# The cached keys of a decode unit turned inside the next slot, between the second and third turned group, instead of at a slot's end

## The chip, the cores and the metric

The kernel runs on one core of one Trainium2 chip. Its time is the device time in microseconds. The kernel before took 1446.33 us (median of 3 runs, 1446.19 to 1446.55).

## What is computed

One inference step of one decoder layer, for a prompt of 512 tokens and 8 decode sequences of one token each with 2048 cached positions. The layer is `x + 1/2 FFN`, then `x + Mixer`, then `x + 1/2 FFN`, and a final norm. The change lies in the mixer's attention (heads of 64 values, 8 query heads, 2 key heads):

```python
s = einsum('btghd,btgnkd->btghnk', q, kg) * scale      # selected blocks of cached or new keys
p = softmax(where(ms, s, NEG));  o_sel = einsum('btghnk,btgnkd->btghd', p, vg)
s = einsum('btghd,bkgd->btghk', q, kw) * scale         # sliding window of 512
p = softmax(where(mw, s, NEG));  o_win = einsum('btghk,bkgd->btghd', p, vw)
return gates[..., 0:1] * o_cmp + gates[..., 1:2] * o_sel + gates[..., 2:3] * o_win
```

The same function serves the prompt, whose keys are the new rows, and the samples, whose keys come from the paged caches and the window buffer. Everything is computed in float32.

## The kernel before

The program is written out engine by engine, with semaphores. It runs FFN 1, the mixer's input projection, the attention stage, the mixer's gates and output projection, and FFN 2. The attention stage, from about 684 to 862 us, is where the change lies. Two kinds of work are interleaved there.

**Prompt units.** There are eight, p = 0 to 7 (four head pairs by two branches). For each, TensorE computes scores (`scores`) into fixed banks, VectorE adds the causal mask, takes maxima and writes them to the tile `sm` (`big_scores`, L1297), ScalarE takes exponentials, VectorE makes factors (`factors`, L1313) and scales two small tiles, and GpSimd scales six tiles of `sm` by the factors (`scaled(p)`, L653; 128x512 twice, 128x384 twice, 128x256, 128x128). TensorE then turns (transposes) the scaled tiles in six groups e = 0 to 5 (`turns`, L1707; labels `("tp", p, e)`); ScalarE copies each out (`turned`, L892) to `ptp` or `ptd`, and TensorE multiplies by the value rows (`values`, L1719).

**Sample units.** There are ten, v = 0 to 9 (two window units, eight batches). The cached rows of unit v lie in `GB[v % 2]`. TensorE turns its keys in four quarters of four 128x128 transposes (`sample_keys`, L1741; labels `("kt", v, q)`), each copied to the tile `kt` by ScalarE (quarters 0 and 2, L852) or, from v = 4, by VectorE (quarters 1 and 3, L1290). Then come its scores (`sample_scores`, L1753; label `sc`), VectorE's addition of the selection mask into `sS`, which empties the bank, and the maximum (L1271), ScalarE's exponential, the turning of `sS` (label `pt`), and its product with the values (`sample_values`; label `pv`), which VectorE copies to `oacc` (L1285) after the factors. GpSimd gathers the rows of unit p + 4 from the cache inside `scaled(p)`, after its second tile, once the values of unit p + 2 are done.

**Slots.** The loop over p = 0 to 6 stands on each engine (ScalarE L942, VectorE L1379, TensorE L1838): a slot turns and multiplies prompt unit p, computes scores and factors of p + 1, and handles sample unit p + 3. Each engine does its queue strictly in order.

**The ring.** Banks 5 to 7 of PSUM are shared by all results named by labels, in the order of the list `RING` (L372 to L384). TensorE takes a bank with `claim` (L1685), which waits until the content three places earlier in the list has been copied away (`emptied`). The list has to follow TensorE's order.

Of the kernel before, what the change touches and what calls it, by code (L numbers as in the profile page):

```python
# [120 lines left out]
def build(nc, a):  # L121

    with ExitStack() as ctx:
# [40 lines left out]
        sc = small("sc", [P, 4, 2, DB])  # L164
# [204 lines left out]
        def keys_of(v):  # L369
            return [("kt", v, q) for q in range(4)]  # L370
# [2 lines left out]
                                                                          ("pt", 1), ("pv", 1)]  # L373
        RING += keys_of(2) + [("kc",), ("sc", 2), ("cs", 0), ("cs", 1), ("pt", 2), ("pv", 2)] + keys_of(3)
        for p_ in range(8):
            RING += [("tp", p_, e) for e in range(3)] + ([("sc", p_ + 3)] if p_ < 7 else []) + [("tp", p_, e) for e in range(3, 6)]
            if p_ == 0:
                RING += [("ct", 0), ("ct", 1)]
            if p_ < 7:
                RING += [("pt", p_ + 3), ("pv", p_ + 3)]  # L380
            if p_ < 6:
                RING += keys_of(p_ + 4)
            if p_ == 6:
                RING += [("st",)]  # L384
        RING += [("fw",), ("os",)]
# [295 lines left out]
        def _(act):  # L681
# [170 lines left out]
            def keys(v, quarters):  # L852

                for q in quarters:
                    act.wait_ge(ring_full, full("kt", v, q))
                    if v:
                        act.wait_ge(ring_full, full("sc", v - 1))
                    act.activation(kt[:, q, :], bank[:, rbank("kt", v, q), :], ACT.Copy).then_inc(ring_act, 1)
# [33 lines left out]
            def turned(p, tiles):  # L892

                for e in tiles:
                    act.wait_ge(ring_full, full("tp", p, e))
                    if e == 0 and p:
                        act.wait_ge(pv_done, p)
                    if e == 0 and p == 0:
                        act.wait_ge(ring_full, full("hid"))
                    g, bk = e % 2, rbank("tp", p, e)  # L900
                    for i in ((3,), (2,), (1, 0))[e // 2]:
                        src = bank[:, bk, (2 * P if i == 0 else 0):][:, 0:(i + 1) * P].rearrange("p (k n) -> p k n", n=P)
                        if g == 0:
                            dst = ptp[:, 0:i + 1, (i + 1) * P:(i + 2) * P]
                        else:
                            dst = ptd[:, :, :].rearrange("p k n -> p (k n)")[:, (3 - i) * 5 * P:(3 - i) * 5 * P + (i + 1) * 6 * P]\
                                .rearrange("p (k n) -> p k n", n=6 * P)[:, :, 0:P]
                        ins = act.activation(dst, src, ACT.Copy)
                    ins.then_inc(ring_act, 1)
# [30 lines left out]
                act.activation(oth[:, j, 0:SEQ], bank[:, 4, :], ACT.Copy).then_inc(o_hi, 1)  # L940

            for p in range(7):  # L942
                turned(p, range(4))
                sample_exp(p + 3)
                turned(p, (4, 5))
                if p == 0:
                    for g in range(KVH):
                        act.wait_ge(ring_full, full("ct", g))
                        act.activation(ptc[:, g, :], bank[:, rbank("ct", g), :], ACT.Copy).then_inc(ring_act, 1)
                exps(p + 1, TOPROW)  # L950
                sample_turned(p + 3)
                exps(p + 1, REST)
                if p < 6:
                    keys(p + 4, (0, 2))
                if p % 2:
                    merged(p // 2)
            hi(U_M3)
# [46 lines left out]
            for t in range(QT + 1):  # L1004
                p = P if t < QT else DB
# [6 lines left out]
        def _(dve):  # L1012
# [229 lines left out]
            turned = bank[0:NCMP, 4, 0:2 * P].rearrange("p (b e) -> p b e", e=32)[:, :, 0:NH]  # L1242
# [28 lines left out]
            def sample_scores(v):  # L1271

                k = stat(v)
                dve.wait_ge(ring_full, full("sc", v))
                if v:
                    dve.wait_ge(ring_full, full("pt", v - 1))
                blocks = mk[:, k, 0:NSEL - 1].unsqueeze(1).unsqueeze(3).to_broadcast([P, 4, NSEL - 1, 4])
                tt(sS[:, :].rearrange("p (s k c) -> p s k c", s=4, c=4), bank[:, rbank("sc", v), :].rearrange("p (s k c) -> p s k c", s=4, c=4),
                   blocks, ALU.add).then_inc(ring_dve, 1)
                dve.wait_ge(*emptied("sc", v))  # L1280
                st.did(dve.tensor_reduce(smx[:, k:k + 1], sS[:, :], AX.X, ALU.max))
                st.wait()
                ts(snm[:, k:k + 1], smx[:, k:k + 1], -SCALE, None, ALU.mult).then_inc(s_nm, 1)
# [6 lines left out]
            def keys(v, quarters):  # L1290

                for q in quarters:
                    dve.wait_ge(ring_full, full("kt", v, q))
                    dve.wait_ge(ring_full, full("sc", v - 1))
                    dve.tensor_copy(kt[:, q, :], bank[:, rbank("kt", v, q), :]).then_inc(ring_dve, 1)
# [81 lines left out]
                tt(otl[:, j, 0:SEQ], bank[:, 4, :], oth[:, j, 0:SEQ].bitcast(F32), ALU.subtract).then_inc(o_lo, 1)  # L1377

            for p in range(7):  # L1379
                sample_scores(p + 3)  # L1380
                big_scores(p + 1)
                factors(p + 1)
                sample_values(p + 3)
                if p < 6:
                    keys(p + 4, (1, 3))
                if p % 2:
                    merged(p // 2)

# [90 lines left out]
        def _(pe):  # L1479
# [227 lines left out]
            def turns(p, tiles):  # L1707
                for e in tiles:
                    g = e % 2
                    out = claim("tp", p, e)  # L1710
                    pe.wait_ge(*((big_p, 6 * p + (1, 2, 3, 4, 6)[e]) if e < 5 else (big_pd, 2 * p + 2)))
                    for i in ((3,), (2,), (1, 0))[e // 2]:
                        for k in range(i + 1):
                            c = (k if g == 0 else i - k) * P + (2 * P if i == 0 else 0)
                            s = (i * (i + 1) // 2 + k) * P
                            ins = turn(out[:, c:c + P], sm[:, g, s:s + P])
                    ins.then_inc(ring_full, 1)
# [118 lines left out]
            sample_keys(3)  # L1836

            for p in range(7):  # L1838
                turns(p, range(3))
                sample_scores(p + 3)  # L1840
                turns(p, range(3, 6))
                scores(p + 1, (3, 2, 0))
                if p == 0:
                    pe.wait_ge(cmp_p, 1)
                    for g in range(KVH):
                        out = claim("ct", g)
                        for i in range(QT):
                            ins = turn(out[:, i * P:(i + 1) * P], cm[:, g, i, :, :].rearrange("p j n -> p (j n)"))
                        ins.then_inc(ring_full, 1)
                sample_turns(p + 3)  # L1850
                scores(p + 1, (1,))
                values(p)
                if p % 2:
                    cmp_values(p // 2)
                sample_values(p + 3)
                if p < 6:
                    sample_keys(p + 4)

            def m3(k, i=None):

# [58 lines left out]
            for t in range(QT + 1):  # L1919
                p = P if t < QT else DB  # L1920
# [68 lines left out]
```

## Time and profile before

| | us |
|---|---|
| median of 3 runs | 1446.33 (1446.19 to 1446.55) |
| the profiled execution | 1445.9 |
| its span, first to last instruction | 1444.1 |
| TensorE busy | 1390.6 |
| VectorE, ScalarE, GpSimd busy | 613.2, 519.9, 566.7 |
| mean granted TensorE clock | 0.984 of full |

The span is what the rows below are measured in; 1.8 us lie around it. Busy times are sums over the whole span, and do not tell which engine is waited for in a stage. GpSimd starts the scaling of a prompt unit at 750.34, 765.18, 779.98, 794.79, 809.59, 824.39 and 838.72 us (p = 1 to 7), which gives the length of a slot.

### The profile page before, as it was taken

What the parts mean: (1) busy time and instruction counts of PE and PEld (TensorE: products, weight loads), DVE (VectorE), ACT (ScalarE), POOL (GpSimd) and SP (SyncE); (2) the same over time, 40 slices, a digit from 0 to 9 for tenths busy, and PEclk for the clock granted to TensorE, in tenths of its full rate; (3) what the DMA queues carried; (4) which work ended last, traced back from release to release, by engine and by line L of the source; (5) the groups of instructions that cost most, each with busy time, mean ns of one, the idle gap of its engine ahead of it and who ended that gap; (6) DMA issues with size and microseconds to landing.
All of it is one profiled execution on the core that took longest, in us unless ns stands there. A gap on an engine that the chain in (4) does not pass through costs nothing.

```text
span 1444.1 us, 27266 instructions
## 1 busy us (share of the span) xinstructions
PE 1390.6 (96%) x11592; PEld 1338.0 (93%) x11592; DVE 613.2 (42%) x920; ACT 519.9 (36%) x803; POOL 566.7 (39%) x290
## 2 busy tenths in 40 slices
PE   7999999999999999999788889998999999999998
PEld 7999999999999999998655569998999999999997
DVE  4677242330224473494366532123853331023362
ACT  5667532221222322222366643323243431122221
POOL 4330344453344434340044635443444454344440
PEclk9999999999999999999789999999999999999999
DMA  8531133322223442325443313223222232133311
GB/s 306 192 116 59 61 100 102 117 88 77 69 87 101 160 146 88 88 61 162 134 144 149 141 50 103 88 87 116 89 88 88 87 131 74 61 99 101 110 37 59
DMA packets 114882, 152.22 MB, mean 105 GB/s; under 512 B 4614, under 2 KB 109290, under 8 KB 112676
## 3 DMA queue, kind: packets, MB, share of 16 engines
q1 hardware_dynamic: 112284, 117.70, 25.5%
q0 software_dynamic: 2304, 33.56, 6.2%
q8 instruction: 46, 0.75, 0.2%
q14 instruction: 16, 0.13, 0.0%
q10 hardware_dynamic: 232, 0.09, 0.0%
HBM read 147.57 MB, written 7.95 MB: 108 GB/s over the span
## 4 chain that ended last, share of the span: by engine, by line
PE 90%; DVE 3%; POOL 3%; ACT 2%; DMA 1%; issue 1%; SPq 0%; ACTq 0%; DVEq 0%
PE bank L1607 74%; PE bank L1549 6%; PE bank L1483 5%; POOL sm L662 2%; PE bank L1702 1%; PE bank L1501 1%; DVE sm L1305 1%; PE bank L1804 1%; PE bank L1729 0%; DMA w<-w_cmpk 0%; ACT sm L888 0%; DVE tmp L1057 0%; POOL GB L576 0%; PE bank L1758 0%; ACT yr L1007 0%
## 5 line engine op out<-in xcount | busy, mean ns | idle before, releaser
L585 POOL TENSOR_TENSOR wlo<-raw,whi 128x1024 fp32r<-128x1024 f32 (+3 forms) x182 | 457.8, 2517 | 647.6 <-ACT whi L706 636.9
L706 ACT ACTIVATE whi<-raw 128x1024 fp32r<-128x1024 f32 (+3 forms) x183 | 196.4, 1076 | 676.4 <-PE bank L1607 670.1
L1607 PE MATMUL bank<-xh,whi 128*128 128x260 f32 (+1 forms) x2032 | 411.8, 284 | 0.5 <-DVE vcS L1033 0.4
L1607 PE MATMUL bank<-xh,wlo 128*128 128x260 f32 (+1 forms) x2032 | 410.8, 284 | 0.0
L1607 PE MATMUL bank<-xl,whi 128*128 128x260 f32 (+1 forms) x2032 | 410.4, 284 | 0.0
L1607 PEld LDWEIGHTS bank<-xh,whi 128*128 128x128 f32 (+1 forms) x2032 | 314.2, 189 | 1.5 <-DVE xl L1064 0.5
L1607 PEld LDWEIGHTS bank<-xh,wlo 128*128 128x128 f32 (+1 forms) x2032 | 313.7, 189 | 0.3
L1607 PEld LDWEIGHTS bank<-xl,whi 128*128 128x128 f32 (+1 forms) x2032 | 313.2, 189 | 0.3
L1116 DVE TENSOR_TENSOR tmp<-bank,rr 128x520 f32<-128x520 f32 x88 | 61.6, 700 | 284.1 <-PE bank L1607 283.6
L1607 PE MATMUL bank<-hl,whi 128*128 128x260 f32 x704 | 142.1, 283 | 0.0
L1607 PE MATMUL bank<-hh,wlo 128*128 128x260 f32 x704 | 141.8, 283 | 0.0
L1607 PE MATMUL bank<-hh,whi 128*128 128x260 f32 x704 | 141.5, 282 | 0.0
L1607 PEld LDWEIGHTS bank<-hh,whi 128*128 128x128 f32 x704 | 108.6, 188 | 0.0
L1607 PEld LDWEIGHTS bank<-hh,wlo 128*128 128x128 f32 x704 | 108.5, 189 | 0.0
L1607 PEld LDWEIGHTS bank<-hl,whi 128*128 128x128 f32 x704 | 108.3, 188 | 0.0
L1123 DVE TENSOR_TENSOR hl<-tmp,hh 128x520 f32 x44 | 90.9, 2065 | 40.3 <-ACT hh L807 40.3
L1130 DVE SCALAR_TENSOR_TENSOR xT<-bank,xT 128x520 f32<-128x520 f32 x32 | 22.4, 700 | 161.1 <-PE bank L1607 161.1
L662 POOL TENSOR_SCALAR sm<-sm,fct 128x512 f32<-128x512 f32 (+3 forms) x48 | 57.8, 1221 | 58.9 <-DVE fct L1324 58.6
L1026 DVE TENSOR_TENSOR XT0l<-bank,XT0h 64x512 fp32r<-64x512 f32 x64 | 44.1, 690 | 27.4 <-ACT XT0h L748 26.3
L1057 DVE TENSOR_TENSOR tmp<-tmp,tmp 128x520 f32<-128x520 f32 x21 | 53.5, 2546 | 0.7
L1026 DVE TENSOR_TENSOR XT1l<-bank,XT1h 64x512 fp32r<-64x512 f32 x64 | 44.2, 690 | 19.8 <-ACT XT1h L748 18.5
L748 ACT ACTIVATE XT0h<-bank 64x512 fp32r<-64x512 f32 x64 | 40.4, 631 | 20.1 <-PE bank L1483 19.0
(319 smaller groups left out, 1749.4 us busy)
## 6 DMA issues: line engine op xcount, KB each, us to landing
raw<-ffn_w_gate SPq DMA_DIRECT2D x22, 1024.0 KB, 5.3
raw<-ffn_w_up SPq DMA_DIRECT2D x22, 1024.0 KB, 5.2
raw<-w_mix_in SPq DMA_DIRECT2D x17, 1024.0 KB, 5.0
raw<-ffn_w_down SPq DMA_DIRECT2D x8, 1536.0 KB, 6.6
raw<-ffn_w_down SPq DMA_DIRECT2D x8, 1280.0 KB, 5.8
GB<-state_win_kv SPq DMA_DIRECT2D x8, 512.0 KB, 5.5
raw<-w_mix_out SPq DMA_DIRECT2D x4, 1024.0 KB, 5.1
win_kv_sample<-state_win_kv SPq DMA_DIRECT2D x1, 4088.0 KB
```

The source lines that it names most:

```text
L585: pool.tensor_tensor(tile(wlo, w, k, u), raw_tile(u), tile(whi, w, k, u).bitcast(F32), ALU.subtract)\
L662: pool.tensor_scalar(v, v, fct[:, g, i:i + 1], None, ALU.mult).then_inc(big_p, 1)
L706: act.activation(dst, src, ACT.Copy).then_inc(hi_done, 1)
L748: ins = act.activation(dst, src, ACT.Copy)
L1026: ins = tt(dst, src, hi_.bitcast(F32), ALU.subtract)
L1057: ins = tt(ssq[:, :], ssq[:, :], tmp[6][:, :], ALU.add)
L1116: tt(two(dst[:, :]), acc(g), two(rr[:, :]), ALU.mult).then_inc(acc_free, 1)
L1123: tt(hl[:, c, :].rearrange("p o t -> p (o t)"), tmp[1 + j][:, :], hh[:, c, :].rearrange("p o t -> p (o t)").bitcast(F32), ALU.subtract).th ...
L1130: stt(two(xT[:, d, :]), acc(g), 0.5, two(xT[:, d, :]), ALU.mult, ALU.add).then_inc(acc_free, 1)
L1483: return pe.transpose(dst, src, ident[0:n, 0:n])
L1549: ins = pe.matmul(hid, w[:, kk, j, :], x[kk][b % 2][:, s, r:r + NCMP, :].rearrange("p c g -> p (c g)"), start=(s + r + n == 0), stop=(s == ...
L1607: ins = pe.matmul(acc(g)[0:m, h, :], w[:, u % WS, c, 0:m], x[:, c, h * HT:(h + 1) * HT], start=(c == 0 and n == 0), stop=(c == k - 1 and n ...
```

## The change

The turning of the keys of unit p + 4 leaves the end of slot p (p = 0 to 5). In its place, slot p (p = 1 to 6) turns the keys of unit p + 3 after groups 0 and 1 and before group 2. The list `RING`, ScalarE's copies of quarters 0 and 2 and VectorE's copies of quarters 1 and 3 move with it.

```diff
         for p_ in range(8):
-            RING += [("tp", p_, e) for e in range(3)] + ([("sc", p_ + 3)] if p_ < 7 else []) + [("tp", p_, e) for e in range(3, 6)]
+            RING += [("tp", p_, e) for e in range(2)] + (keys_of(p_ + 3) if 0 < p_ < 7 else []) + [("tp", p_, 2)] + ([("sc", p_ + 3)] if p_ < 7 else []) + [("tp", p_, e) for e in range(3, 6)]
...
             if p_ < 7:
                 RING += [("pt", p_ + 3), ("pv", p_ + 3)]
-            if p_ < 6:
-                RING += keys_of(p_ + 4)
@@ ScalarE
             for p in range(7):
-                turned(p, range(4))
+                turned(p, range(2))
+                if p:
+                    keys(p + 3, (0, 2))
+                turned(p, range(2, 4))
                 sample_exp(p + 3)
                 turned(p, (4, 5))
...
                 exps(p + 1, REST)
-                if p < 6:
-                    keys(p + 4, (0, 2))
                 if p % 2:
                     merged(p // 2)
@@ VectorE
             for p in range(7):
+                if p:
+                    keys(p + 3, (1, 3))
                 sample_scores(p + 3)
                 big_scores(p + 1)
                 factors(p + 1)
                 sample_values(p + 3)
-                if p < 6:
-                    keys(p + 4, (1, 3))
                 if p % 2:
                     merged(p // 2)
@@ TensorE
             for p in range(7):
-                turns(p, range(3))
+                turns(p, range(2))
+                if p:
+                    sample_keys(p + 3)
+                turns(p, (2,))
                 sample_scores(p + 3)
                 turns(p, range(3, 6))
...
                 sample_values(p + 3)
-                if p < 6:
-                    sample_keys(p + 4)
```

## Rows read from the trace of the kernel before

**Rows 1.** The page: its first line, and TensorE's busy time

```profile
span 1444.1 us, 27266 instructions
...
PE 1390.6 (96%) x11592; PEld 1338.0 (93%) x11592; DVE 613.2 (42%) x920; ACT 519.9 (36%) x803; POOL 566.7 (39%) x290
```

**Rows 2.** Chain that ended last, slot 3: start us, us, what

```profile
779.98 3.10 POOL sm L662 x2
...
784.33 3.95 POOL sm L662 x4
...
788.42 0.85 PE bank L1483 x6
789.26 1.93 PE bank L1702 x12
...
794.53 0.17 DVE fct L1324
...
794.79 3.10 POOL sm L662 x2
```

**Rows 3.** TensorE's timeline, slot 3: start, us, instructions, idle before, releaser

```profile
780.88 1.09 PE L1483 MATMUL bank<-ident,GB 128*128 128x128 f32 x8
783.67 1.09 PE L1483 MATMUL bank<-ident,GB 128*128 128x128 f32 x8 [1.70 <-DVE oacc L1288]
784.60 1.65 PE L1483 MATMUL bank<-ident,sm 128*128 128x128 f32 x11
786.19 1.06 PE L1758 MATMUL bank<-kt,qp 128*32 128x512 f32 x8
...
788.42 0.85 PE L1483 MATMUL bank<-ident,sm 128*128 128x128 f32 x6 [0.69 <-POOL sm L662]
```

**Rows 4.** Chain that ended last, slots 1 and 6

```profile
754.88 2.42 PE bank L1483 x19
757.30 1.00 PE bank L1758 x8
...
828.41 2.42 PE bank L1483 x19
830.84 0.99 PE bank L1758 x8
...
832.65 0.55 PE bank L1483 x3
```

**Rows 5.** Timelines of ScalarE and VectorE, slot 3: key copies, sample scores

```profile
784.37 0.60 ACT L858 ACTIVATE kt<-bank 128x512 f32<-128x512 f32 x1 [1.82 <-PE bank L1483]
...
784.81 0.69 DVE L1295 COPY kt<-bank 128x512 f32<-128x512 f32 x1 [0.59 <-PE bank L1483]
787.32 0.69 DVE L1278 TENSOR_TENSOR sS<-bank,mk 128x512 f32<-128x512 f32 x1 [1.82 <-PE bank L1758]
```

**Rows 6.** Timelines of GpSimd (slots 3, 6) and VectorE (slot 6)

```profile
784.33 1.27 POOL L662 TENSOR_SCALAR sm<-sm,fct 128x384 f32<-128x384 f32 x1
...
830.84 0.59 POOL L662 TENSOR_SCALAR sm<-sm,fct 128x128 f32<-128x128 f32 x1
...
831.90 0.69 DVE L1278 TENSOR_TENSOR sS<-bank,mk 128x512 f32<-128x512 f32 x1 [0.98 <-PE bank L1758]
```

**Rows 7.** Stretches: length, busy by engine, granted clock, DMA; one chain row

```profile
847.00:848.00 1.00, 1.00 (x7) 1.00 (x6) 0.82 (x5) 0.31 (x1) 0.00 (x0) 0.50 0.00 0
...
849.00:850.00 1.00, 1.00 (x11) 1.00 (x10) 0.00 (x0) 0.00 (x0) 0.00 (x0) 1.00 0.00 0
...
782.00:785.40 3.40, 1.73 (x15) 1.68 (x16) 2.64 (x7) 1.30 (x4) 3.21 (x3) 1.00 0.35 63
...
690.80:692.50 1.70, 1.69 (x10) 1.43 (x8) 0.00 (x0) 1.23 (x3) 0.00 (x0) 0.72 0.27 53
...
688.29 3.85 PE bank L1483 x18
```

**Rows 8.** DMA issues from 740 to 900 us: count, size, us to landing

```profile
GB<-cache_sel_kv,idx POOLq DMA_INDIRECT x5, 8.7
```

## The prediction

> **What bounds the kernel now.** I read the page first, then the chain of waits through the mixer's attention stage, then the engines' own timelines inside one slot of it. The page shows TensorE busy for 1390.6 of 1444.1 us [rows 1]: nearly all of the kernel is dense matrix work that the change does not touch. The change acts only between about 750 and 833 us, where seven slots (p = 0 to 6) run at a fixed pace. In the chain of a middle slot (p = 3) the reader is to see who sets that pace [rows 2]: GpSimd scales six score tiles from 779.98 to 788.28 us, with one gather between them. TensorE turns the last two groups at 788.42, the scores of the next head follow at 789.26, VectorE reduces them and makes the factors until 794.70, and GpSimd starts again at 794.79. The period is 794.79 - 779.98 = 14.81 us. No piece of that chain is a turning of cached keys.
>
> TensorE's timeline in the same slot says the same from the other side [rows 3]. It does two quarters of keys at 780.88, stands still 1.70 us until VectorE has emptied the bank of the sample values, and resumes at 783.67 with the other two quarters, then groups 0 to 2, then the sample scores at 786.19. It stands still again, 0.69 us, before the turning at 788.42, and there it waits for GpSimd. So in this slot TensorE has 0.69 us of room, and the 1.70 us of idle time costs nothing.
>
> Slots 1 and 6 are different [rows 4]. In both the chain goes from the resumed key turning (754.88, 828.41) to the sample scores (757.30, 830.84), and in slot 6 on through VectorE's addition into sS to the turning of group 5 at 832.65. Slot 1 starts its keys late, slot 6 has no gather and so an earlier GpSimd. In these two, whatever delays the sample scores delays the slot.
>
> **The change, part by part.** It removes nothing and adds no instruction. Per unit it moves 16 transposes (four quarters of four), two ScalarE copies, two VectorE copies and their places in the order of the three shared banks. It issues no DMA; SyncE and the gathers on GpSimd keep their places and their conditions (values of earlier units). A gather lands 8.7 us after its issue [rows 8]: the one between the tiles that end at 783.08 and start at 784.33 at about 792, well before its keys are turned in either order. For each of slots p = 1 to 6 the order on TensorE goes from "keys, groups 0, 1, 2, sample scores" (the keys at the end of the slot before) to "groups 0, 1, keys, group 2, sample scores". VectorE's two copies move only past the odd slots' `merged`, which waits for a ScalarE copy that now comes earlier.
>
> Because a bank is claimed only when its content three claims earlier has been copied away, the claims change too: key quarter 0 now needs the sample values emptied (before it was quarter 2), quarters 1 and 2 need groups 0 and 1, quarter 3 needs quarter 0, group 2 needs quarter 1, and the sample scores need quarter 2. The sample scores also need the copy of quarter 3, as before; but before, three groups lay between, and now only group 2 does. That is the new wait. Behind it on TensorE are group 3, then groups 4 and 5 and the scores of the next head; VectorE waits for the sample scores with all of `big_scores` behind them.
>
> Working for slot 3, from its own rows. A quarter takes (784.60 - 783.67) / 2 = 0.465 us of TensorE; its copy starts 784.37 - 784.135 = 0.24 us after it on ScalarE and 784.81 - 784.60 = 0.21 us on VectorE, and takes 0.60 or 0.69 us [rows 3, 5]. Group 1 can start when GpSimd's second tile is done, 779.98 + 3.10 = 783.08, plus the 0.14 us seen between 788.28 and 788.42 [rows 2]: 783.22, and it ends at 783.69. That lies beside the wait for the sample values, which also ended at 783.67: this is where groups 0 and 1 are hidden. Then quarters 0 to 3 run 783.69 to 785.55 (quarter 3 needs quarter 0 copied: 784.16 + 0.24 + 0.60 = 785.00, in time). Group 2 needs GpSimd's third tile, 784.33 + 1.27 = 785.60 [rows 6], plus 0.14, and it was at this moment before too. The copy of quarter 3 ends at 785.55 + 0.21 + 0.69 = 786.45, and with 0.06 us to TensorE (slot 6's addition ends 831.90 + 0.69 = 832.59, group 5 starts at 832.65 [rows 4, 6]) the sample scores start at 786.5, where they started at 786.19 [rows 3]: 0.3 us later. The addition into sS, which began at 787.32 [rows 5], begins near 787.65 and ends near 788.35, and group 5, which needs that bank, is due only after group 4, at 788.42 + 0.35 = 788.77. So 0.35 us of room is left and slots 2 to 5 (four) cost nothing. If that cover were gone, each would cost what the sample scores are late beyond 0.7 us.
>
> ScalarE's exponential of the sample and its copies of groups 4 and 5 move by the same 0.3 us and still end before the exponentials of the next head, which cannot begin before VectorE's first maxima. The key copies lie beside GpSimd's tiles in either order. The 128x384 tile that a VectorE key copy overlaps now takes 1.27 us [rows 5, 6], and the two of that shape with the rest of the group take 3.95 us together [rows 2], so one beside a copy cannot cost more than some hundredths more. (The Trainium skill's page SBUF — State Buffer, section Who interferes with whom, says that a VectorE copy in a two-port mode shuts GpSimd out until it ends. By that, two copies of 0.69 us in the middle of GpSimd's chain could cost up to 1.4 us a slot, 5.5 us in four slots. The 1.27 us tile does not agree for these copies, which read PSUM.)
>
> Slots 1 and 6: the keys resume at 754.88 and 828.41 in either order, since both begin with the emptied sample values, and groups 0 and 1 are done by then. Before, quarters 2 and 3, groups 0 to 2 lay ahead of the sample scores: 757.30 - 754.88 = 2.42 and 830.84 - 828.41 = 2.43 us [rows 4]. Now it is 4 x 0.465 + 0.21 + 0.69 + 0.06 = 2.82, and with the 0.05 us by which quarter 3 may have to wait for quarter 0's copy 2.87 us. That is 0.45 us more in each of the two slots. GpSimd gives nothing back in slot 6: its last tile ends at 831.43 [rows 6], already ahead of group 5 at 832.65.
>
> Sum: 2 x 0.45 + 4 x 0 = +0.9 us. The next part of the kernel takes back some of it. From 845 us on TensorE runs at the lower of its two levels, 1.2 GHz: granted 0.50 at 847 us with 7 instructions a microsecond, 1.00 (2.4 GHz) at 849 us with 11 [rows 7]. TensorE had been nearly idle before. If that stretch ends at the same time of the span and the work enters it 0.9 us late, 0.9 us of it is spent on nothing that would have run at 7/11 of the speed: 0.9 x (1 - 7/11) = 0.33 us back. If it goes with the work, nothing comes back. Bounds 0 and -0.33; I take -0.2, near the middle, as one execution cannot tell. The sum is +0.7 us: the profiled execution's 1445.9 us (its span of 1444.1 and 1.8 around it) would be 1446.6, and on the median of 1446.33, which lies 0.43 above the profiled one, it gives 1447.0 us. I forecast a time that can't be told from that of before: 0.2% is 2.9 us, about what a measurement of this kernel can tell from no change.
>
> **The rivals.** First: the three fresh ring waits are dearer than a stream of turns, so that the sample scores become the bound in every slot. Place: the wait for quarter 3's copy. It decides from 0.7 us of delay of the sample scores. At 0.2 us more for each of quarter 3, group 2 and the sample scores, the delay in slots 2 to 5 is 0.3 + 0.6 = 0.9, hence a little over 0.2 us lost in each, and 1.05 in slots 1 and 6: +2.9 us; at 0.3 us more each, 0.5 x 4 + 1.35 x 2 = +4.7 us. That is 1449.2 to 1451.0, slower. For it: the sample scores do wait for a copy directly now, and semaphore steps of up to 0.24 us are in the rows. Against it: those steps are already in my sum.
>
> Second: the idle time is truly removed, and the slot shortens. This needs TensorE to be the bound, which holds only in slot 6, where GpSimd would allow groups 4 and 5 at 831.43 + 0.14 = 831.57, while group 5 came at 832.65, and to a smaller part in slot 1. If the copies ran hidden and TensorE saved what it waits, at most 0.7 us in slot 6 and 0.1 in slot 1: -0.8 us, 1445.5. Against it: the wait for the sample values stands at the same moment, since VectorE does the factors first.
>
> Third: the clock falls inside the slots. The trace shows it at 1.00 in the emptiest piece of a slot, 782.0 to 785.4, with 1.73 us of work [rows 7]. At the lower level 7 instructions take the place of 11, so keys, group 2 and sample scores, 3 us of work, would take 4.7: 1.7 less 0.35 of room is 1.3 us each time, in one to four slots +2 to +6 us with my sum: 1448.3 to 1452. For it: the transposes now lie in one stretch from 781 to 786.5 us instead of to 786.2. Against: in the stage's start 18 transposes ran from 688.29 us with nothing else and the clock rose among them (0.72 in 690.8 to 692.5) [rows 7], so turning keeps the clock. (The Trainium skill, TensorE: Matmul & The Clock Gate, Part 4: PE-mode transpose, states that transposing does not count as busy for the gate. By that rule the longer stretch would speak against this change; the rise among transposes speaks against the rule here.)
>
> Fourth: the low stretches near 845 and 862 us move against the work and one vanishes or one is added: 3.4 us at 7/11 is 1.2 us either way, so 1445.8 or 1448.2. Fifth: the order is not the bound anywhere and nothing moves: 1446.3, within the forecast's own spread.
>
> **How the numbers follow.** Forecast (+0.2 to +1.6 us, the fifth case in it) 0.70; first rival 0.09; second 0.07; third 0.06; fourth 0.08. Beyond 2.9 us slower lie most of the first, half of the third and a little of the fourth: 0.11. Faster by over 2.9 us needs the second with both low stretches gone: 0.04. Same: 0.85. The range takes the second rival at its bound with one low stretch gone (-0.8 - 0.5) and the first at its start: 1445.0 to 1449.4.
>
> **What would show it.** In the changed kernel's trace: groups 0 and 1 near 781.7 and 783.2 us of slot 3; one short wait before quarter 0 and one of about 0.4 us before the sample scores, released by VectorE's key copy; in slots 2 to 5 still a wait of TensorE for GpSimd before group 4, shorter or equal, and a period of 14.8 us; in slots 1 and 6 a period longer by 0.4 to 0.5 us; granted clock 1.00 throughout the slots. The prediction is wrong if the period of slots 2 to 5 moves by over 0.1 us, if slot 6 shortens, or if the clock drops there.

## The result and the profile after

The changed kernel takes 1454.07 us (median of 5 executions, 1448.1 to 1455.16), the kernel before, on the same chip, 1446.55 us (5 executions, 1446.19 to 1448.51). The ratio is 1.0041 with an interval of 1.0025 to 1.0057. It is slower, by about 6 us, where a time that can't be told from that of before was forecast, with 1449.4 us as the upper end. Of the executions below one, of a later kernel, took 1976.95 us at a mean clock of 0.641, and is left out of that kernel's mean and ratio.

The first thing to see on the page is that TensorE is busy for longer, 1400.5 against 1390.6 us [rows 1], with the same number of instructions. No work was added, so the same products took longer. The line of the granted clock (tenths of full speed in 40 slices, here of 36 us) has a 6 in the 20th slice, where the page of before has a 7, and an 8 in the 24th, from 835 to 871 us, where the page of before has a 9 (its line ran `...99999789999...`, with its 8 in the 21st).

```profile
span 1452.2 us, 27266 instructions
...
PE 1400.5 (96%) x11592; PEld 1345.4 (93%) x11592; DVE 613.3 (42%) x920; ACT 521.5 (36%) x803; POOL 566.6 (39%) x290
...
PEclk9999999999999999999699989999999999999999
```

The lines below are the chain that ended last (start us, us, what), slots 1 to 3. They answer to [rows 2] and [rows 4]; source lines are one or two lower in this kernel. "Turning row" is a row of transposes (L1482).

```profile
756.20 1.99 PE bank L1482 x16
758.19 0.02 issue
758.21 0.70 DVE kt L1294
758.91 0.14 issue
759.05 1.07 PE bank L1757 x8
...
766.99 3.10 POOL sm L660 x2
...
771.34 3.95 POOL sm L660 x4
775.28 0.14 issue
775.42 0.85 PE bank L1482 x6
776.27 1.92 PE bank L1701 x12
...
781.79 3.11 POOL sm L660 x2
784.90 0.14 issue
785.04 4.09 PE bank L1482 x20
789.12 0.03 issue
789.15 0.70 DVE kt L1294
789.85 0.14 issue
789.99 1.06 PE bank L1757 x8
...
797.93 3.10 POOL sm L660 x2
```

Slot 2 is the slot of [rows 2] again: GpSimd, the turning, the scores, and a period of 781.79 - 766.99 = 14.80 us. Slots 1 and 3, and slot 6 too, have something that no chain of before has: VectorE's copy of a key quarter (L1294) stands between the turning and the sample scores. Slot 3 takes 16.14 us. Its turning row has 20 transposes in 4.09 us, 0.20 us each, where that of slot 1 has 16 in 1.99 us, 0.12 each. The reason is in the granted clock (stretch, length, busy time by engine, clock, DMA):

```profile
782.30:785.70 3.40, 1.75 (x28) 1.18 (x18) 1.45 (x5) 2.17 (x10) 3.25 (x3) 1.00 0.00 0
785.70:789.10 3.40, 3.40 (x17) 3.40 (x17) 0.69 (x1) 1.79 (x3) 3.36 (x4) 0.50 0.68 198
846.00:854.00 8.00, 5.88 (x28) 5.65 (x29) 4.13 (x20) 2.15 (x4) 4.17 (x4) 0.57 0.26 91
863.00:875.00 12.00, 12.00 (x64) 12.00 (x65) 1.82 (x4) 5.58 (x8) 4.85 (x3) 0.57 0.14 45
```

At 785.7 us the clock goes to its lower level, 1.2 GHz, for 3.4 us. What TensorE did ahead of it is on its timeline (start, length, instructions, idle before and releaser):

```profile
781.67 1.08 PE L1772 MATMUL bank<-GB,pT 128*32 128x128 f32 x32
783.50 0.63 PE L1482 MATMUL bank<-ident,sm 128*128 128x128 f32 x4 [0.74 <-POOL sm L660]
785.04 0.63 PE L1482 MATMUL bank<-ident,sm 128*128 128x128 f32 x4 [0.91 <-POOL sm L660]
785.57 3.54 PE L1482 MATMUL bank<-ident,GB 128*128 128x128 f32 x16
```

Where [rows 3] had eight key transposes and one wait of 1.70 us, there are now two waits, 0.74 and 0.91 us, with four transposes between them, and narrow products (32 columns of weights) ahead. That alone does not make the clock fall: when the changed kernel was traced again, the same slot had the same two waits (0.75 and 0.91 us) and the same busy time (1.74 us in 3.4 us), and the clock stayed at 1.00:

```profile
780.90:784.30 3.40, 1.74 (x30) 1.18 (x22) 1.45 (x5) 2.27 (x9) 3.25 (x3) 1.00 0.00 0
784.30:787.70 3.40, 3.04 (x28) 2.15 (x27) 1.38 (x2) 2.22 (x4) 3.36 (x4) 1.00 0.67 193
...
782.19 0.63 PE L1482 MATMUL bank<-ident,sm 128*128 128x128 f32 x4 [0.75 <-POOL sm L660]
783.73 0.63 PE L1482 MATMUL bank<-ident,sm 128*128 128x128 f32 x4 [0.91 <-POOL sm L660]
```

The other two rows of the changed kernel's stretches show the low stretches after the slots, longer than in the profile of before: 6.8 us from 847 on and 10.2 us from 864 on, where before it was 3.4 and 3.4.

The 8.1 us between the two spans divide as follows (from the starts of the same instructions in both traces): 1.2 us before slot 1, where the kernels are alike and only the low stretches lie differently; 0.57 us in slot 1; 1.34 in slot 3; 0 in slots 2, 4 and 5; 0.57 in slot 6; 4.0 between unit 7's first scaling and the output projection; 0.4 in the output projection.

### The profile page after: what moved, and what is told of

Read it like the earlier page. It is cut to its first block, busy times and chain, and to the rows that moved or that the text cites. A ratio compares the mean times of both kernels' runs of the same rounds, so it can differ in the third digit from the quotient of the medians.

```text
span 1452.2 us, 27266 instructions
## 1 busy us (share of the span) xinstructions
PE 1400.5 (96%) x11592; PEld 1345.4 (93%) x11592; DVE 613.3 (42%) x920; ACT 521.5 (36%) x803; POOL 566.6 (39%) x290
## 4 chain that ended last, share of the span: by engine, by line
PE 90%; DVE 3%; POOL 2%; ACT 2%; issue 1%; DMA 1%; SPq 0%; ACTq 0%; DVEq 0%
PE bank L1606 74%; PE bank L1548 6%; PE bank L1482 5%; POOL sm L660 2%; PE bank L1701 1%; PE bank L1500 1%; ACT sm L886 1%; DVE sm L1304 1%; PE bank L1803 1%; DMA w<-w_cmpk 0%; PE bank L1757 0%; DVE tmp L1056 0%; PE bank L1772 0%; PE bank L1728 0%; POOL GB L574 0%
## 5 line engine op out<-in xcount | busy, mean ns | idle before, releaser
L1129 DVE SCALAR_TENSOR_TENSOR xT<-bank,xT 128x520 f32<-128x520 f32 x32 | 22.4, 700 | 161.1 <-PE bank L1606 161.1
```

The costliest lines, as they stand in the source:

```text
L1129: stt(two(xT[:, d, :]), acc(g), 0.5, two(xT[:, d, :]), ALU.mult, ALU.add).then_inc(acc_free, 1)
```

## The experiments

Single executions of one kernel differ by up to 9 us, and in the traces the low stretches (at the lower clock) lie otherwise from one to the next. So averages and ratios count here, and a trace shows one case among several. Mostly it is a mild one: in 15 of the 19 rows below that were timed with their profile, the traced execution is faster than the mean of its kernel, for ten transposes in slot 6 by 4.8 us. Each ratio comes with its interval, and microseconds are worked out from it (0.001 is 1.45 us). "Old order" is the kernel before, "new order" the changed one. The traces are compared by three sums in us, taken from the starts of the same instructions: slots (GpSimd's first tile of unit 1 to that of unit 7), after (from there to the first product of the output projection), and projection (from there to its last product). The kernel before, run beside each of them, had means of 1446.9 to 1447.5 us.

| kernel | ratio (interval) | mean of executions | slots | after | projection |
|---|---|---|---|---|---|
| kernel before, first profile | | | 88.38 | 162.57 | 48.07 |
| control, old order | 1.0005 (0.9996 to 1.0013) | 1448.0 | 88.39 | 162.89 | 48.15 |
| changed | 1.0041 (1.0025 to 1.0057) | 1452.9 | 90.86 | 166.55 | 48.48 |
| changed, again | 1.0034 (1.0020 to 1.0049) | 1451.8 | 89.53 | 163.82 | 48.61 |
| new order in 2 to 5 | 1.0015 (1.0001 to 1.0029) | 1449.7 | 88.37 | 162.56 | 48.05 |
| new order in 1 and 6 | 1.0034 (1.0020 to 1.0048) | 1451.8 | 89.53 | 163.96 | 48.68 |
| changed, products as fillers in 1 to 6 | 1.0035 (1.0022 to 1.0048) | 1452.5 | 92.22 | 163.97 | 48.72 |
| changed, transposes as fillers in 1, 3, 5 | 1.0025 (1.0014 to 1.0036) | 1450.6 | 89.55 | 164.00 | 48.74 |
| new order in 1 | 1.0018 (1.0009 to 1.0026) | 1449.8 | 88.95 | 162.52 | 48.15 |
| new order in 6 | 1.0010 (0.9999 to 1.0020) | 1448.7 | 88.94 | 162.61 | 47.94 |
| new order in 2 and 4 | 1.0001 (0.9992 to 1.0010) | 1447.7 | 88.33 | 163.02 | 48.21 |
| new order in 3 and 5 | 1.0018 (1.0006 to 1.0029) | 1449.6 | 88.37 | 162.96 | 48.20 |
| old order, +10 transposes in 6 | 1.0052 (1.0031 to 1.0073) | 1453.4 | 89.43 | 163.99 | 48.71 |
| old order, +20 in 6 | 1.0043 (1.0029 to 1.0056) | 1452.8 | 90.55 | 166.53 | 48.43 |
| old order, +29 in 6 | 1.0020 (1.0008 to 1.0032) | 1449.9 | 91.54 | 162.87 | 48.15 |
| old order, +10 in 1 | 1.0031 (1.0015 to 1.0047) | 1451.5 | 89.47 | 166.95 | 48.72 |
| new order, +19 in 6 | 1.0037 (1.0024 to 1.0049) | 1452.0 | 91.60 | 162.98 | 48.17 |
| filled old order | 0.9972 (0.9961 to 0.9982) | 1443.5 | 88.39 | 161.07 | 46.06 |
| filled old order, +10 in 6 | 0.9999 (0.9990 to 1.0008) | 1446.7 | 89.54 | 162.65 | 46.08 |
| filled new order | 0.9994 (0.9985 to 1.0003) | 1446.5 | 89.50 | 164.28 | 46.08 |

### Which slots cost

The changed kernel again, and the new order in part of the slots:

```diff
-                if p:
-                    sample_keys(p + 3)
+                if p in (2, 3, 4, 5):      # and (1, 6), (1,), (6,), (2, 4), (3, 5)
+                    sample_keys(p + 3)
...
                 sample_values(p + 3)
+                if p < 6 and p + 1 not in (2, 3, 4, 5):
+                    sample_keys(p + 4)
```

The same choice stands in the list of the ring and in the loops of ScalarE and VectorE.

> The changed kernel unaltered, to see how much of its 7.5 us is bound to the order and how much to the execution. Theory A (fixed cost and clock): the period of slots 2 to 5 is 14.8 us wherever the granted clock is 1.00, slots 1 and 6 are each 0.5 to 0.6 us longer than before, together +1.1 us in every execution; the rest is stretches at the lower level, which come in most executions of this order: median 1450 to 1455 us, with one execution or another near 1448. Theory B (chance): the rest was a bad draw, and the kernel lands at 1447.5 to 1449 with as little spread as the kernel before. Theory C (ring waits in every slot): periods of 15.2 us or more in slots 2 to 5 at full clock.

> Only slots 2 to 5 take the new order, slots 1 and 6 keep the old one. Theory A: the fixed cost of 1.1 us is gone (all slots have the old length at full clock), but the low stretches inside a slot stay possible, since they follow from the two short waits with four turns between them in slots 3 and 5: 1446.5 where the clock holds, 1447.5 to 1453 where it falls. Theory B: 1446.5. Theory C: at least +1.6 us in every execution.

> Only slots 1 and 6 take the new order. Theory A: +1.1 us at full clock, two slots of 0.5 to 0.6 us more, the clock at 1.00 in slots 2 to 5 in every execution: 1447.3 to 1449. Theory B: the same 1447.5. Theory C: less than +1 us, since the cost would lie in the other four slots.

Again, the changed kernel cost 4.9 us (2.9 to 7.1); its single executions went from 1447.7 to 1454.7, so it was no bad draw. Slots 2 to 5 were 14.80 us each in this trace, which takes theory C away. Slots 1 and 6 were 15.42 and 14.90 us, +1.15 us together, as in every trace that has them with no added work on their chain. But only slots 1 and 6 in the new order cost 4.9 us (2.9 to 6.9), not the 1.15 that theory A gave them: a miss. Slots 2 to 5 alone cost 2.2 us (0.1 to 4.2).

> Only slot 1 takes the new order. In the earlier runs slots 1 and 6 together cost 1.15 us of slot length, but 4.7 us on average. Theory A (a clock fall in a slot whose start has two waits with four turns between): slot 1 has both waits (0.86 and 0.75 us), so in part of the executions the clock falls behind it; average +2.5 to +4 us over the kernel before, 0.6 of it slot length. Theory D (what matters is where the slots end against the low stretches near 845 and 862 us): slot 1 shifts the end by 0.6 us and gets about half of the 4.7.

> Only slot 6 takes the new order. It comes behind an odd slot, so products of the compressed values run until just before its first group, and it has no second long wait. Theory A: +0.6 us of slot length and no clock fall in it: average +0.6 us (within 1 us of it, given the spread of the executions). Theory D: +2 us or more, as for slot 1, or all of it if only the last slot's form counts.

> Only slots 2 and 4 take the new order; both come behind an odd slot. Theory A: slot lengths of 14.8 us, clock 1.00 in them, average within 1 us of the kernel before. Theory E (any slot of the new order can lose its clock): half of the 2.5 us that slots 2 to 5 cost together.

> Only slots 3 and 5 take the new order; both come behind an even slot and have the two waits of 0.74 and 0.91 us. Theory A: all of the 2.5 us that slots 2 to 5 cost on average, as +1.3 us for each fall, in part of the executions. Theory E: half of it. If the profiled execution shows a fall, it begins within 785 to 790 us or 815 to 820 us.

Slots 2 and 4 cost nothing (0.1 us, -1.2 to 1.4), slots 3 and 5 cost 2.6 us (0.9 to 4.2): as theory A said, though the two intervals just leave room for theory E's 1.25 us each. Slots 3 and 5, like slot 1, are the ones whose group 0 finds TensorE waiting, since no products of the compressed values come before it. Slot 1 cost 2.6 us (1.3 to 3.8) with 0.57 us of slot length, slot 6 1.4 us (-0.1 to 2.9). None of these four traces has a fall inside slots 1 to 6. So a fall in a slot has been seen once, in the trace of the changed kernel (mean granted clock 0.977), and that slots 3 and 5 are its place is indicated, not shown. The mean clock of every execution points there too. It is 0.976 or 0.977 in 2 of 5 and 4 of 10 executions of the changed kernel, in 3 of 12 with the new order in slots 2 to 5 and in 2 of 12 with it in 3 and 5; in none of 47 with it in slots 1, 6, 1 and 6, or 2 and 4; and in none of the 146 of the kernel before that were timed beside the experiments. Those with it took 1452.3 to 1455.5 us, 5 to 8 us more than the kernel before and not 1.3. But only one of them was traced, and 6 of 30 executions of the delayed old order below have such a clock too, so this is an indication as well.

### Filling the waits inside the slots

```diff
             for p in range(7):
-                turns(p, range(2))
+                pe.wait_ge(big_rd, 8 * (p + 1))
+                if p in (3, 5):
+                    busy(5)                  # 5 transposes of ident into bank 2, read by nobody
+                turns(p, (0,))
+                if p in (1, 3, 5):
+                    busy(6)
+                turns(p, (1,))
+                if p == 1:
+                    busy(5)
```

A first form had products in place of transposes, four and five of them in each of slots 1 to 6:

> The changed kernel with work that nobody reads in TensorE's two waits at the start of slots 1 to 6: four 128x128 products ahead of group 0 and five between groups 0 and 1, 0.47 and 0.58 us in waits of 0.74 and 0.91 us. Theory A: the granted clock stays at 1.00 from 750 to 843 us, the loss of 1.3 us in a slot is gone, and what stays is 1.1 us fixed plus what the stretches before and after the slots add: 1447.5 to 1452. Theory B: no difference from the changed kernel. Theory C: slower than the changed kernel by some tenths, as TensorE has less room.

> The changed kernel with transposes that nobody reads, each 0.117 us, sized to TensorE's waits in slots 1, 3 and 5 alone: five ahead of group 0 and six between groups 0 and 1 in slots 3 and 5, six between groups 0 and 1 and five ahead of the keys in slot 1. The first filled kernel used products that took nearly twice as long as assumed and lengthened slots 2, 4 and 6 by 0.9 us each; these are meant to fit. Theory A (clock falls behind the two waits): slot periods as in the changed kernel (15.4, then 14.8, 14.9 in slot 6), no fall in a slot, and the average comes down from the changed kernel's 1451.9 to 1448 to 1449.5, near the 1.15 us of slot length above the kernel before. If filling does nothing for the clock: 1451 to 1453.

The first form came to 1.0035 (1.0022 to 1.0048). Its products took about 0.22 us each (two records of 0.11), twice the time of a transpose, and the periods of slots 2, 4 and 6 went to 15.7 us. It had no fall in slots 1 to 6, but its own cost hides what that gave. The second form fits: its periods are those of the changed kernel (15.42, four of 14.81, 14.90), the clock stayed at 1.00 in the slots, and the ratio is 1.0025 (1.0014 to 1.0036), 3.6 us. That is 1.3 us below the changed kernel, within what the two intervals leave open, and not the 1448 to 1449.5 us expected: its mean is 1450.6. So falls in the slots are not the whole of the rest; nor does its trace show that the fillers kept the clock, since the changed kernel's second trace has 1.00 in the slots without them. Its trace loses a further 1.4 us in the stretch after the slots and 0.7 us in the projection, against the first profile of the kernel before, with the clock at full speed in all slots.

### Delaying the end of the slots

That surplus stood in every trace whose slots ended some 1.15 us later. So the old order was delayed by a known amount and otherwise left alone: transposes that nobody reads, on the chain of slot 6, ahead of the next scores. The expectations count 0.117 us for each; in the traces they follow each other by 0.11 us, and the slots grew by 1.0, 2.2 and 3.1 us for 10, 20 and 29.

```diff
                 turns(p, range(3, 6))
+                if p == 6:
+                    pe.wait_ge(big_rd, 8 * (p + 1))
+                    for _ in range(10):      # and 20, 29; or p == 1
+                        turn(bank[:, 2, 0:P], ident[:, :])
                 scores(p + 1, (3, 2, 0))
```

> The kernel before with ten transposes that nobody reads (1.17 us) in slot 6 ahead of the next head's scores, on the chain. Theory F (a later end of the slots meets the low stretches worse): +2.3 to +3.5 us on average, the slots 1.2 us longer and the rest between unit 7 and FFN 2. Theory G (a delay costs itself): +1.2 us.

> The same with twenty transposes, 2.34 us. Theory F: not twice the cost of ten, since the alignment changes again: anything from +1.5 to +5 us, with a surplus over 2.34 us that differs from that of ten. Theory G: +2.3 us.

> The same with 29 transposes, 3.39 us, the length of the shortest low stretch in the traces (3.4 us). Theory F: work and low stretches lie to each other as in the kernel before, so the surplus is gone: +3.4 us, within 0.7. Theory G: +3.4 us as well; it differs from F at ten and twenty only.

> Ten transposes in slot 1 instead of slot 6, 1.17 us. Theory F: as ten in slot 6, +2.3 to +3.5 us, since the slots between keep a fixed length at full clock and only the end's shift counts. Theory G: +1.2 us. A clear difference between the two places would speak for a cost made inside the slots.

A delay of 1.0 us cost 7.5 us (4.5 to 10.6; 6.3 by the means, of six executions), one of 2.2 us 6.2 us (4.2 to 8.1), and one of 3.1 us only 2.9 us (1.2 to 4.6). Ten transposes in slot 1, 1.1 us, cost 4.5 us (2.2 to 6.8). Ten transposes cost even more than theory F gave them, and none of it is additive: by the means 29 cost 2.9 us less than 20 and 3.5 us less than ten, more than the scatter of the executions explains. The traces show where. With 29 transposes the stretch after the slots takes 162.87 us and the projection 48.15, as in the control (162.89 and 48.15); with 10 it takes 163.99 and 48.71, with 20 166.53 and 48.43. For ten all this adds up to 2.7 us in the traced execution, the fastest of its six; where the others lose more was not traced. Here are the same stretches of the old order (control), then of 20 transposes, then of 29; columns as above.

```profile
861.00:866.00 5.00, 5.00 (x32) 5.00 (x32) 1.13 (x3) 3.14 (x5) 1.58 (x1) 0.68 0.31 103
866.00:871.00 5.00, 5.00 (x43) 5.00 (x43) 0.70 (x1) 3.89 (x6) 4.51 (x4) 0.98 0.03 9
```

```profile
861.00:866.00 5.00, 5.00 (x25) 5.00 (x25) 0.00 (x0) 0.00 (x0) 0.00 (x0) 0.50 0.33 105
866.00:871.00 5.00, 5.00 (x25) 5.00 (x26) 1.12 (x3) 4.90 (x7) 3.37 (x2) 0.53 0.00 0
```

```profile
861.00:866.00 5.00, 5.00 (x43) 4.40 (x39) 0.69 (x1) 0.60 (x1) 2.05 (x1) 1.00 0.36 101
866.00:871.00 5.00, 5.00 (x30) 5.00 (x30) 1.13 (x3) 4.80 (x7) 3.27 (x2) 0.66 0.01 3
```

Control: a low stretch, then full speed (43 instructions in 5 us). With 20: low for the whole 10 us, 25 instructions in each half. With 29: the same one low stretch as in the control, some 3.3 us later. TensorE is busy all this time in each of them. In the control the clock fell behind the narrow products of the samples' output (8 columns, L1886 and L1889 of the kernel before; they run from 859.05 to 862.6 us, the fall is at 862.8), and only the dense products behind them were slow for one stretch. With 20 it fell at 860.5, inside the narrow products (from 859.70 on), which then lasted until 865.8 us, and it stayed low. The changed kernel again has a longer low time too:

```profile
861.00:866.00 5.00, 5.00 (x31) 5.00 (x31) 1.13 (x3) 2.00 (x4) 0.41 (x1) 0.65 0.33 108
866.00:871.00 5.00, 5.00 (x31) 5.00 (x30) 0.00 (x0) 4.29 (x5) 5.00 (x3) 0.67 0.00 0
```

All twenty traces follow one pattern. With 3.4 us of low clock from about 862 us on, the stretch after the slots is 162.5 to 163.0 us long (nine traces); with 6.8 us, 163.8 to 164.0 (five); with 10.2 us, and 6.8 more near 845 us, 166.5 to 166.9 (three). In the filled kernels of the next part, with no low stretch near 845 us, 3.4, 6.8 and 10.2 us go with 161.1, 162.7 and 164.3. So each further 3.4 us of low clock at this place costs 1.2 to 2.0 us, and a delay of 1 us can bring one of them or two.

The last two runs turned this on the new order itself, and on the filled kernel of the next part:

> The changed kernel with nineteen transposes that nobody reads (2.22 us) on the chain of slot 6, so that its slots end 1.15 + 2.22 = 3.4 us later than before. Theory F: more work, yet not slower than the changed kernel's average of 1451.9: 1449.5 to 1452, with few executions above 1453 and these by falls in slots 1, 3 and 5. Theory G: 1454.

The new order with 2.1 us more work on its chain came to 1.0037 (1.0024 to 1.0049), mean 1452.0, where the changed kernel had 1.0041 and 1.0034 and means of 1452.9 and 1451.8. The added work cost nothing that can be told, and its trace has 162.98 and 48.17 us after the slots, the control's sums. A cost that only adds up would have put it at 1454, which is at the edge of what its six executions allow.

### Filling the waits outside the slots

If low stretches are what costs, the old order can gain too. Its TensorE waits in slot 0 (1.85 and 1.42 us), in unit 7 (1.69 and 1.66 us) and ahead of the output projection (4.6 us).

```diff
+            pe.wait_ge(big_rd, 64)
+            turns(7, (0,))
+            busy(12)
+            turns(7, (1,))
+            busy(12)
+            turns(7, (2,))
             m3(0)
...
+            pe.wait_ge(acc_free, group(U_M4) - WS + 1)
+            busy(36, acc(group(U_M4))[:, 0, 0:P])
             for j in range(DC):
                 unit(U_M4 + j, mh, ml, ready=ml_done if j == 0 else None)
```

In slot 0, `busy(12)` stands ahead of group 2 and `busy(10)` ahead of group 4.

> The kernel before, unaltered, as a control of the spread: the ratio lies at 1.000 within 0.001, single executions between 1443.5 and 1451.7 us, and its trace has the granted clock at 1.00 from 750 to 840 us wherever the low stretches elsewhere fall. A fall inside slots 1 to 6 here would speak against theory A.

> The kernel before, old order, with transposes that nobody reads in four long waits outside slots 1 to 6: 12 and 10 in slot 0's waits for GpSimd (1.85 and 1.41 us), 12 and 12 in the waits of unit 7 (1.69 and 1.66 us), 36 in the 4.6 us of idle time ahead of the output projection. If the level of the clock follows what TensorE does, the low stretches near 845 and 999 us go: 6.8 us at the lower level cost up to 3.4 us, 3.4 us cost up to 1.5 us, and the fall in slot 0 costs 2.5 us where it comes. Average 1441 to 1444 us against 1447. If transposes do not hold the clock: 1447, or up to 1 us slower.

> All fillers of the two others together on the new order: what is left between this and the filled old order is the new order's own slot length, 1.15 us, if the clock was the rest: average 1.0 to 2.0 us over the filled old order. If the new order costs the rest by another way, the difference stays at 4 to 5 us.

> The filled old order (average 1443.5) with ten transposes (1.17 us) on the chain of slot 6. The low stretches near 845 and 999 us are filled there, the one near 862 us is not. Theory F: between +1.2 and +3 us over the filled kernel, by the 862 us stretch alone, so less than the 6 us that the same delay cost in the unfilled kernel. Theory G: +1.2 us.

The filled old order is the fastest kernel of the study: median 1443.53 us against 1447.2 of the kernel before on the same chip, ratio 0.9972 (0.9961 to 0.9982), and its executions lie within 1442.7 to 1444.6. The page, the four stretches and the filled wait:

```profile
span 1441.8 us, 27430 instructions
...
844.00:851.00 7.00, 6.64 (x55) 6.40 (x56) 3.68 (x18) 2.15 (x4) 3.72 (x4) 1.00 0.22 74
861.00:866.00 5.00, 5.00 (x31) 5.00 (x31) 1.12 (x3) 3.35 (x5) 1.78 (x1) 0.66 0.24 83
...
998.00:1008.00 10.00, 9.27 (x80) 9.06 (x78) 7.87 (x11) 4.58 (x9) 2.34 (x1) 1.00 0.40 130
...
996.22 4.09 PE L1483 MATMUL bank<-ident 128*128 128x128 f32 x36
1001.04 0.47 PE L1607 MATMUL bank<-mh,whi 128*128 128x260 f32 x2 [0.73 <-DVE ml L1462]
```

The control, for the same places:

```profile
844.00:851.00 7.00, 6.05 (x35) 6.05 (x36) 2.34 (x16) 1.93 (x4) 2.35 (x3) 0.63 0.02 6
...
998.00:1008.00 10.00, 6.51 (x37) 6.54 (x38) 7.40 (x9) 4.17 (x8) 2.77 (x2) 0.66 0.42 143
```

The low stretches near 845 and 999 us are gone (1.00 against 0.63 and 0.66), the projection takes 46.06 us instead of 48.15, and what is left is the stretch at 861 us, which nothing filled. The 82 added transposes cost nothing that the trace shows: they lie in waits, TensorE still waits 0.73 us behind the last 36, and GpSimd's first tile of unit 1 starts at 751.57 us, within the 748.3 to 752.5 of the traces without them.

The filled new order came to 0.9994 (0.9985 to 1.0003), 1446.5 us on average: 3.0 us over the filled old order, where 1 to 2 were expected. 1.1 of it is slot length. The trace has 3.2 us more in the stretch after the slots (164.28 against 161.07), at the one place left unfilled, and 1.55 us less ahead of slot 1, where the two kernels are alike. The filled old order with ten transposes in slot 6 (1.15 us of slot length) came to 0.9999 (0.9990 to 1.0008), 3.2 us over it in the means (3.9 by the two ratios), a little over the 3 expected, and again with the surplus in that stretch (162.65). So with two of three low places filled, a delay still costs nearly three times itself, and the trace puts it at the third.

The control came to 1.0005 (0.9996 to 1.0013) and its slots had the clock at 1.00 throughout.

## Why the prediction was wrong

**What bounds the kernel, the ring, slots 2 to 5: right.** GpSimd's chain kept its 14.80 us in slots 2, 4 and 5 of the changed kernel and in all four in the second trace. In slot 3 of the second trace the sample scores came 6.63 us after GpSimd's start, against 6.21 before: 0.42 us later, where the sum had 0.3. TensorE's wait for GpSimd before group 4 went from 0.69 to 0.26 us, so the cover was thinner than worked out, and enough. At full clock none of these slots was slowed by the fresh waits; the first rival (dearer ring waits) did not come. The gathers stayed hidden.

**Slots 1 and 6: right in mechanism, a little small.** 0.45 us each was the sum, 0.57 us each was measured, in every trace without added work in the slot. The chain shows the term: sample scores at 759.05 behind a key turning from 756.20 is 2.85 us where I had 2.87. That this agrees so closely is in part luck: the end of the key copy took 0.14 us to reach TensorE, not the 0.06 of the sum, and the rest was about as much shorter. What I had wrong is the start and the end. After the emptied sample values TensorE resumed 0.14 us later, where it resumed 0.05 us later in the old order, and I had taken the resumption as unchanged; the sample scores themselves took 1.07 us where they took 1.00.

**GpSimd beside the key copies: right.** GpSimd's four smaller tiles took 3.95 us in slot 2, as in [rows 2], with both key copies moved beside them.

**The clock inside the slots: weighed and set too low.** The third rival said that the clock falls in a slot at 1.3 us each. It came in slot 3 of the first trace, with 1.34 us. I gave it 0.06 because turning alone had raised the clock at 688 us and because the emptiest stretch of a slot had 1.73 us of work at full speed. I did not look at what the new order would put beside the waits: narrow products, 0.74 us of waiting, four transposes, 0.91 us of waiting, with the first two key quarters gone behind the waits. Whether that is what tipped it is not shown: the 3.4 us ahead of the fall have 1.75 us of work, as much as the stretch that I had read, and slot 3 in the same order kept the clock in seven other traces (three of them with fillers there). Of the two theories on turning, the traces keep the row's: 36 transposes held the clock ahead of the projection, in all three filled kernels. (The Trainium skill's rule in TensorE: Matmul & The Clock Gate, Part 4: PE-mode transpose, that the gate does not count transposing as busy in the same way, does not agree with these float32 runs: 1.00 over 998 to 1008 us with the 36 transposes, 0.66 in the control without them.)

**The clock after the slots: the step that failed.** The sum credited 0.2 us, between bounds of 0 and 0.33, to work that enters a low stretch late, and the fourth rival allowed 1.2 us either way. Both treated the low stretches as something that a later start can only shorten or hit by chance. In the trace of the changed kernel the slots take 2.5 us more, the stretch from unit 7 to the output projection is longer by 4.0 us, and the projection by 0.4: +4.4 us where the sum had -0.2, the largest part of the 8.1 us between the spans. The delayed old order shows that it needs no new order: slots that take 1.0 to 1.1 us more cost 4.5 to 7.5 us there, and 1.1 to 4.1 us of it stand in the same stretch of their two traces and 0.6 in the projection. So the term is the largest of all, and it has the other sign. The price of one more low stretch was in the fourth rival (1.2 us; the later windows, with 25 instead of 43 instructions in 5 us, give about 1.4). What the prediction lacked is that a delay of the size of its own sum would mostly bring one or two more, at several places, and its chance of 0.08 for this rival was far too low.

**The spread.** I had three executions of the kernel before, within 0.4 us, and took their median for the kernel's time to a few tenths. The comparisons later had executions of it from 1443.4 to 1451.7 us. The range of the forecast, 1445.0 to 1449.4, was no wider than the spread of the unchanged kernel.

**What stays open.** How often the clock falls inside slots 1, 3 and 5, and what decides it: one fall was seen in the eight traces that have slots 3 and 5 in the new order, three of these with fillers there, while slots 3 and 5 alone cost 2.6 us (0.9 to 4.2). Where the slower executions, which were not traced, lose their time. And why a delay costs more on average than a random position against the low stretches would. The position is not random: of the 17 traces with slot 0 unfilled, the low stretch near 862 us begins 112.0 to 112.8 us after GpSimd's first tile of unit 1 in 14, and 115.3 to 115.9 us after it in the three whose slots end over 3 us later, as if the work before set it; no run tested that.

## What to carry to other kernels

Where TensorE's clock falls after a stage of waits, a change of one microsecond ahead of it is not worth a microsecond: it can decide how much low time the next dense work meets, so look up each fall of the granted clock behind the edit and price one more of each before summing. Look at what an edit takes out from beside a wait, and not only at the length of the wait. Waits that cannot be removed can be filled: transposes that nobody reads, sized to each wait, made this kernel 0.28% faster and its executions more alike (within 1.8 us of each other), without touching its order.

## What the runs showed of the hardware

- Transposes alone kept the clock up: 36 of them in a wait of 4.6 us held the granted clock at 1.00 where it had been 0.66 over 10 us, and the work that followed took 2.0 us less.
- A stretch of 16 float32 products with 8 columns, 0.22 us each, as long as one with 128 columns, was followed by the lower level (1.2 GHz) although TensorE was busy all the time (859.05 to 862.6 us in the control, the fall at 862.8; busy 5.00 of 5.00 us from 861 to 866, clock 0.68).
- A plain 128x128 product of float32 took about 0.22 us, a transpose of the same size 0.11 us at the higher level and 0.21 us at the lower.
- A wait's end reached TensorE 0.05 us after VectorE's copy in one order and 0.14 us in another, for the same pair of instructions.
